# Sixteen-expert transformer kernel: one expert's down product split, a lighter residual, a turned branch, and small moves in order at the start, the merge and the last norm

## The reference, cut to what matters

```
mod = silu(c) @ w_ada + b_ada                     # 9 rows of 1024
h = x + 0.5*gt1 * swiglu(modulate(rms(x), sh1, sc1))          # 1024 -> 2*2816 -> 1024
h = h + gt2 * token_mixing(modulate(rms(h), sh2, sc2))        # pooling + dilated attention
h = h + 0.5*gt3 * swiglu(modulate(rms(h), sh3, sc3))
x = rms(h) * g_final
for l in range(2):
    mix = concat(retention, sliding window, latent attention) @ w_out[l]
    x = layer_norm(ALPHA * x + mix)               # ALPHA = 4 ** 0.25
    # router: best of 4 groups of 4 experts, then its 2 best experts
    y = sum over experts of gate * (silu(x@Wg) * (x@Wu)) @ Wd  # 16 experts, 1024 -> 2*256 -> 1024
    x = layer_norm(ALPHA * x + y)
```

## Time and profile before

| | |
|---|---|
| median of 3 runs | 1162.05 us (1161.95 to 1162.21) |
| the profiled execution, its own time | 1163.61 us |
| its span, first to last record | 1161.8 us |
| granted TensorE clock, mean | 0.985 of full speed |
| instructions | 25234 |
| TensorE busy | 95% of the span |
| VectorE, ScalarE, GpSimd busy | 76%, 54%, 8% |
| moved by DMA | 271.95 MB, mean 234 GB/s |

### The profile page before, as it was taken

How to read it: one execution, slowest core, us unless ns; L and a number is a source line. 1 busy time by engine, 2 the same in 40 slices (tenths; PEclk the granted TensorE clock), 3 DMA queues, 4 the chain that set the end, 5 groups by cost and what they waited for, 6 DMA issues and landing times.

```text
span 1161.8 us, 25234 instructions
## 1 busy us (share of the span) xinstructions
PE 1106.2 (95%) x10870; PEld 850.9 (73%) x10870; DVE 879.8 (76%) x1109; ACT 629.2 (54%) x782; POOL 90.2 (8%) x104
## 2 busy tenths in 40 slices
PE   4899999999999899999999999999999999999995
PEld 4777776698787487777688785887759777588772
DVE  4799799789775775556667857999956775799994
ACT  1554344453465554344466446777746644677762
POOL 1115511071000100000000000000000000000000
PEclk9799999899999999999999999999999999999997
DMA  9999799466544577665464225599985333479970
GB/s 341 371 369 374 245 351 357 145 223 201 187 167 161 171 251 267 217 217 154 141 199 148 75 72 222 206 383 407 381 264 168 112 109 99 194 279 387 399 317 36
DMA packets 134430, 271.95 MB, mean 234 GB/s; under 512 B 9396, under 2 KB 98072, under 8 KB 126008
## 3 DMA queue, kind: packets, MB, share of 16 engines
q1 hardware_dynamic: 123960, 231.79, 56.4%
q0 software_dynamic: 7904, 29.25, 7.1%
q10 hardware_dynamic: 2464, 9.44, 2.1%
HBM read 269.41 MB, written 1.05 MB: 233 GB/s over the span
## 4 chain that ended last, share of the span: by engine, by line
PE 72%; DVE 14%; ACT 7%; DMA 4%; issue 3%; ACTq 0%; SPq 0%; DVEq 0%
PE ps L750 57%; DVE wlo L470 7%; ACT whi L445 2%; DMA area<-in_w_ada_dram 2%; PE ps L1642 2%; DMA raw<-in_w_in_dram 1%; PE ps L888 1%; PE ps L1238 1%; PE ps L1268 1%; PE ps L906 1%; PE ps L1278 1%; DVE x L2262 1%; PE ps L1522 1%; PE ps L1075 1%; PE ps L1267 1%
## 5 line engine op out<-in xcount | busy, mean ns | idle before, releaser
L470 DVE SCALAR_TENSOR_TENSOR wlo<-raw,whi 128x2048 f16<-128x2048 f32 (+4 forms) x212 | 466.1, 2231 | 49.2 <-ACT whi L445 48.4
L445 ACT ACTIVATE whi<-raw 128x2048 f16<-128x2048 f32 (+4 forms) x212 | 384.6, 1848 | 26.2 <-DMA raw<-in_w_ffn_in_dram 10.2
L750 PE MATMUL ps<-uhi,whi 128*128 128x256 f16 (+2 forms) x1328 | 330.8, 261 | 0.9 <-DVE ulo L2317 0.4
L750 PE MATMUL ps<-ulo,whi 128*128 128x256 f16 (+2 forms) x1328 | 330.6, 261 | 0.0
L750 PE MATMUL ps<-uhi,wlo 128*128 128x256 f16 (+2 forms) x1328 | 330.5, 261 | 0.0
L750 PE MATMUL ps<-whi,hreg 128*128 128x512 f16 (+1 forms) x656 | 204.8, 381 | 0.2 <-DVE area L2897 0.2
L750 PE MATMUL ps<-area,whi 128*128 128x96 f16 (+2 forms) x2168 | 154.9, 210 | 3.2 <-ACT area L2157 3.2
L750 PEld LDWEIGHTS ps<-area,whi 128*128 128x128 f16 (+2 forms) x2168 | 145.4, 99 | 15.4 <-issue 9.0
L750 PE MATMUL ps<-area,wlo 128*128 128x96 f16 (+2 forms) x1084 | 149.4, 210 | 0.0
L750 PEld LDWEIGHTS ps<-uhi,whi 128*128 128x128 f16 (+1 forms) x1328 | 130.8, 98 | 23.4 <-issue 9.0
L750 PEld LDWEIGHTS ps<-ulo,whi 128*128 128x128 f16 (+1 forms) x1328 | 130.6, 98 | 15.4 <-issue 1.7
(11 more groups left out here) (361 smaller groups left out, 1428.0 us busy)
## 6 DMA issues: line engine op xcount, KB each, us to landing
raw<-in_exp_w_gate_up_dram SPq DMA_DIRECT2D x64, 1024.0 KB, 7.6
raw<-in_w_ffn_in_dram SPq DMA_DIRECT2D x44, 1024.0 KB, 7.3
raw<-in_w_in_dram SPq DMA_DIRECT2D x34, 1024.0 KB, 7.1
area<-in_w_ada_dram POOLq DMA_DIRECT2D x48, 512.0 KB, 7.3
raw<-in_w_ffn_out_dram SPq DMA_DIRECT2D x22, 1024.0 KB, 8.0
raw<-in_exp_w_down_dram SPq DMA_DIRECT2D x22, 1024.0 KB, 7.8
raw<-in_w_out_dram SPq DMA_DIRECT2D x12, 1024.0 KB, 5.5
x<-in_exp_w_down_dram SPq DMA_DIRECT2D x6, 1024.0 KB, 5.5
```

Of the source, the lines that this page charges most:

```text
L445: act.activation(whi[:, u.slot, 0:n], raw[:, u.slot, 0:n], ACT.Copy, scale=SW)\
L470: dve.scalar_tensor_tensor(out=wlo[:, u.slot, 0:n], in0=raw[:, u.slot, 0:n], scalar=SW, in1=whi[:, u.slot, 0:n], op0=ALU.mult, op1=ALU.sub ...
L750: last = pe.matmul(o, st, mv, start=start and i == 0, stop=stop and i == 2, skip_group_check=True)
```

## The change

- **A, expert 14.** WHOLE loses expert 14: its down weights come as one more 1 MB unit of the ring in each layer, with a hi and a lo part and float16 matmuls. Expert 15 gets place 3 in WHOLE.
- **B, residual.** The factor is S/SX, which one float16 number holds exactly; ALPHA is divided out of what is added to it, and of the epsilon. Sixteen matmuls per tile instead of 24.
- **C, start.** The three broadcasts go to the pool queue behind its wait for ada_pe >= 2. SP waits for the second block's third piece in the order of loading (`ada_in[1][1]`) before the first two weight units. On PE `ada_direct(1)` comes before `transposes(0)`.
- **D, merge.** The lo part of mixing unit 26 (`unit1(23)`) comes after j = 1 of the merge on DVE, and not before j = 0; the hi part of unit 27 (`unit1(24)`) after j = 1 on ACT, and not after j = 3. Five filler matmuls stand before the second `token_transposes`.
- **E, router.** Twenty filler matmuls become 6; 4 more stand after the first gather. ACT gathers after one hi part instead of four; DVE gathers before `gates()`. PE's branch is turned: `sparse()` is the If body, `dense()` the Else body. The 8 fillers behind the branch become 9 at the end of `sparse()`.
- **F, last norm.** The last layer makes no xn: DVE takes (x - mean) * lng on four halves of 512 columns straight from PSUM, then reciprocal, times it plus lnb per half. The output is stored in four halves.

```diff
-WHOLE = (3, 7, 11, 14, 15)
+WHOLE = (3, 7, 11, 15)
...
-    small[:, C_EPSLN + 1] = LN_EPS * S * S
+    small[:, C_EPSLN + 1] = LN_EPS * S * S / (ALPHA * ALPHA)
...
-            sp.dma_start(posi, a["positions"][0].partition_broadcast(P)).then_inc(rows_in, 16)
-            sp.dma_start(sinks[:, :], a["swa_sinks_2"].rearrange("l h -> (l h)").partition_broadcast(P)).then_inc(rows_in, 16)
-
-            sp.dma_start(rbias[:, :], a["router_bias_2"].partition_broadcast(P)).then_inc(rows_in, 16)
-
             def phase(ph):
+                if ph is ffn1:
+                    sp.wait_ge(ada_in[1][1], 16)
...
             for t in range(TT):
-                sp.wait_ge(x_new, 12 + t + 1)
-                sp.dma_start(out[0, t * P:(t + 1) * P, :], x[:, t, :]).then_inc(out_done, 16)
-            sp.wait_ge(out_done, 32)
+                for hf in range(2):
+                    c = slice(hf * HALF, (hf + 1) * HALF)
+                    sp.wait_ge(x_new, 12 + 2 * t + hf + 1)
+                    sp.dma_start(out[0, t * P:(t + 1) * P, c], x[:, t, c]).then_inc(out_done, 16)
+            sp.wait_ge(out_done, 64)
...
             pool.wait_ge(ada_pe, 2)
+            pool.dma_start(posi, a["positions"][0].partition_broadcast(P)).then_inc(rows_in, 16)
+            pool.dma_start(sinks[:, :], a["swa_sinks_2"].rearrange("l h -> (l h)").partition_broadcast(P)).then_inc(rows_in, 16)
+            pool.dma_start(rbias[:, :], a["router_bias_2"].partition_broadcast(P)).then_inc(rows_in, 16)
...
                                 pe.wait_ge(mod_cols, 4)
+                                if q == 1:
+                                    stay_warm(5, 7)
                                 token_transposes(q, 1)
...
-                    for i, (st, mv) in enumerate(((uhi, res_hi), (ulo, res_hi), (uhi, res_lo))):
-                        pe.matmul(o, st[:, k, xs], mv, start=k % 4 == 0 and i == 0, stop=False, skip_group_check=True)
+                    for i, st in enumerate((uhi, ulo)):
+                        pe.matmul(o, st[:, k, xs], res_one, start=k % 4 == 0 and i == 0, stop=False, skip_group_check=True)
...
-            pe.wait_ge(diag_made, 3)
+            ada_direct(1)
+            pe.wait_ge(diag_made, 2)
             transposes(0)
-            ada_direct(1)
...
-                stay_warm(20, 0)
+                stay_warm(6, 0)
...
                     first_gather()
+                    stay_warm(4, 7)
...
                     scatter(3)
+                    if l < LAYERS - 1:
+                        stay_warm(9, 7)
...
-                with pe.If(count > SLOTS):
+                with pe.If(count < SLOTS + 1):
+                    sparse()
+                with pe.Else():
                     dense()
-                with pe.Else():
-                    sparse()
                 if l < LAYERS - 1:
-                    stay_warm(8, 7)
                     token_transposes(2 * l + 4, 0)
                     stay_warm(9, 7)
...
                                ACT.Copy).then_inc(m_hi, 1)
+                if j == 1:
+                    unit1(24)
             act.activation(flag[:, 6:7], zero8[:, 0:1], ACT.Sqrt)
-            for i in range(24, N_MIX):
+            for i in range(25, N_MIX):
                 unit1(i)
...
-                act.activation(mixhi[:, 2 + p, :], ps[:, 6, 0:T], ACT.Copy, scale=SX).then_inc(yo_hi, 1)
+                act.activation(mixhi[:, 2 + p, :], ps[:, 6, 0:T], ACT.Copy, scale=SX / ALPHA).then_inc(yo_hi, 1)
...
-                emit(4)
+                emit(1)
                 gather(0)
+                emit(3)
...
                 for t in range(TT):
                     token_std(2 * l + 1, t)
-                    token_norm(2 * l + 1, t)
+                    if l < LAYERS - 1:
+                        token_norm(2 * l + 1, t)
...
-            unit = np.float32(ALPHA * S / SX)
-            hi = np.float16(unit)
-            for i, value in enumerate((1.0, float(hi), float(np.float16(unit - np.float32(hi))))):
+            for i, value in enumerate((1.0, S / SX)):
                 dve.tensor_scalar(diag[:, i, :], ident, value, None, ALU.mult).then_inc(diag_made, 1)
...
             mix_out_lo(3)
-            unit1(23)
             for j in range(4):
...
                                   mhi[:, 2 * j:2 * j + 2, :], ALU.subtract).then_inc(m_lo, 1)
+                if j == 1:
+                    unit1(23)
...
+                gather(0)
                 gates()
-                gather(0)
                 emit(1)
...
             for t in range(TT):
-                dve.wait_ge(xn_made, 14 + t + 1)
-                dve.wait_ge(xa_made, 12 + t + 1)
-                link(dve.tensor_tensor(x[:, t, :], xn[:, t, :], lng, ALU.mult))
-                dve.tensor_tensor(x[:, t, :], x[:, t, :], lnb, ALU.add).then_inc(x_new, 1)
+                dve.wait_ge(var_made, 2 * (2 * LAYERS - 1) + t + 1)
+                for hf, c in enumerate(halves):
+                    ins = dve.scalar_tensor_tensor(out=x[:, t, c], in0=ps[:, 2 * t + hf, :], scalar=stat[:, 8 + 4 * t:9 + 4 * t],
+                                                   in1=lng[:, c], op0=ALU.subtract, op1=ALU.mult)
+                link(ins)
+            for t in range(TT):
+                dve.wait_ge(rms_made, 2 * (2 * LAYERS + 3) + t + 1)
+                link(dve.reciprocal(stat[:, 4 + t:5 + t], stat[:, 2 + t:3 + t]))
+                for c in halves:
+                    dve.scalar_tensor_tensor(out=x[:, t, c], in0=x[:, t, c], scalar=stat[:, 4 + t:5 + t], in1=lnb[:, c],
+                                             op0=ALU.mult, op1=ALU.add).then_inc(x_new, 1)
```

24 lines of the change are left out of this document (14 added, 10 removed).

## The result

The changed kernel took **1148.89 us** (median of 4 runs, 1148.26 to 1150.29) beside 1162.0 us for the kernel before (median of 4, 1156.76 to 1162.21). Over the runs of both the ratio is 0.990, 95% interval 0.987 to 0.9929. Six later runs of the changed kernel gave 1147.11 us and 0.9869 (0.985 to 0.9888). So by these ratios the change is worth 12 to 15 us, where 19.1 were forecast: right in sign, too high in size. The predicted range of 1136 to 1150 us is 0.978 to 0.9896 of the time before: the first ratio lies just outside it, the later one inside, and the interval of the first takes in both sides.

The account below looks back on a forecast made before the run. PE, busy 95% of the span, was taken to bound the kernel, with DMA full and DVE 90% busy in the experts. Terms summed to -19.1 us off 1162.05, giving 1143.0 us; range 1136 to 1150.

Parts of the forecast that it names:

- C, start: At the kernel's start: columns for the first product near 37.4 us against 39.62, -2.3 us; bounds -3.6 and +1.4.
- Rival 3: Start does not gain: modulation's second block no faster alone, unit 0 late; +1.4 for -2.3, 1146.7 us; chance 0.12.
- D, merge and clock: Lo parts after the merge end near 390.6, -1.9 us; fillers keep the clock for transposes before FFN2, -1.5 us.
- B, residual: Eight fewer matmuls per tile, -0.45 us each tile: -1.8 in the mixers, -0.9 in each expert stage.
- E, router: At the router: branch costs 0.1 to 0.2 us, first gather from 726.3, -3.5 us per layer; bounds 0 and -3.7.
- The cover in the experts: In the expert stages: DVE's lead of 3.9 us is gone, new waits +0.5 us per layer; bounds 0 and +3.5.
- Rival 1: Experts bound by DVE or DMA: another 1.5 us per layer comes back, 1146.0 us; chance 0.15.
- The jump: End of layer 0's sparse body: jump over the dense body delays the next transposes, +1.1 us; bounds 0 and +3.3.
- A and F: Expert 14's split product -0.85 us per layer, layer 0's wait -0.7; last norm -2.0, last store -0.5.
- Rival 5: Slower: fewer router fillers let the clock fall to 1.2 GHz through the experts; about 1239 us; chance 0.03.

Follow-up runs that it names:

- b1: The kernel before with part C alone: 1161.84 us beside 1162.64, ratio 0.9994 (0.9977 to 1.0011).
- b2: The kernel before with the branch turned alone, its 20 fillers and 8 behind the branch kept: 1169.31 us, ratio 1.0059.
- c3: The changed kernel without the five fillers ahead of the transposes before FFN2: 1147.45 us.
- c2: The changed kernel with the lo part of expert 1's down weights cut to 128 of 2048 columns in both layers: 1143.04 us, ratio 0.9838.
- a1: The changed kernel run again, unaltered: 1146.75 us, ratio 0.9876.
- c1: The changed kernel with DVE's halves product before the sums in FFN1's tenth chunk and expert 1's down weights kept float32: 1143.19 us, ratio 0.9838.
- b3: The changed kernel with DVE's halves product before the sums in FFN1's tenth chunk and three group outputs before the next lo part: 1145.91 us.
- a4: The changed kernel with TensorE's untaken dense body cut to one matmul: 1144.64 us beside 1146.75.
- d2: The kernel of c1 in five rounds beside the changed kernel: 1141.96 us beside 1147.11, ratio 0.9825.

## Why the prediction was wrong, step by step

The sum was 19.1 us and the two spans differ by 13.4. In this pair of traces the missing 5.7 are 2.3 at the start, 2.3 in layer 0's experts, 2.1 in layer 1 and 0.75 at the jump, less 1.8 that the merge, the router and expert 14 gave beyond their terms. Two terms failed: the start's -2.3, taken as kept to the end, and the experts' cover, +0.5. The 0.2% that the text gave a measurement were too few as well: the first interval reaches 0.3% to each side.

- **C, start** (-2.3, got 0 in this pair, a little over 1 us in the mean of the traces; b1: 0.9994). The step that failed is the cover, not the arithmetic of the transfers. The fold starts at 32.99 where 32.7 were worked out. That the first product is 4.35 us earlier, and not 2.3, has two other reasons: the fold takes 2.26 us at clock 1.00 where it took 3.57 at 0.50, and the lo part does not hold the columns, since unit 0 is there at 30.84 and not at 33.2. (PE's transposes were not done before the fold, as the text has it: they run from 29.54 to 33.19, and the fold follows them.) But the text followed PE alone from there: it never asked whether DVE, 76% busy over the span, had the gain too. DVE lost 2.75 of its 4.36 us between 42 and 58 us, waiting for hi parts whose weights had not come (DMA share 1.06), and was 1.68 us earlier at the tenth chunk, with 2.9 us of modulation sums ahead of what ACT and PE wait for. Rival 3's outcome (no gain of the start) came true, by another cause than its own.
- **D, merge and clock** (-3.4, got -4.14). Right: the lo parts end at 390.0 (forecast 390.6), the first transposes are 2.5 us sooner, the second take 1.09 us. The clock's 1.5 us hold for this pair of traces; without the fillers the clock falls in three of four traces (the kernel before, b2 and c3, but not b1), so part of this hit is luck of the pair.
- **B, residual.** 16 matmuls in 0.89 us, as forecast.
- **E, router** (-3.5, got -4.33 in layer 0). The branch is 0.08 us where 0.1 to 0.2 was expected, and ACT's earlier gather saved a further 0.9 us behind it, which the text had counted as nothing. b2 shows how much of this hangs on the parts beside the branch.
- **The cover in the experts** (+0.5 per layer, got a wait of 2.56 us at expert 5 in each, and a stretch of low clock behind it in one): the term that was most wrong. The lead was read right (3.9 us against 4.4 gained), but the new wait was taken as the difference of the two at one lo part. DVE was gapless from the gather to expert 5, and the first group's output stands behind a 2.3 us lo part there. Rival 1, at 0.15, named DVE's pace or DMA, with 1.5 us per layer more; c2 shows that it is DVE and not DMA.
- **The jump** (+1.1, got +1.85). Mechanism right, size low: 4.94 us where the price of the old branch, 3.58, was taken. It starts 0.98 us before the scatter's end (0.4 was taken), and varies from 3.5 to 5.9 us; from the last scatter to the transposes the eleven traces need 0.4 to 2.8 us more than the kernel before, 1.7 in the mean.
- **A and F** as forecast: -1.82 for -1.55 in layer 0, -0.84 for -0.85 in layer 1, -2.5 for -2.5 at the end. In F the four SBUF halves took 0.71 us each and not 0.62; -2.0 had been taken for a sum that gave 2.3, and hit.

In layer 1 the wait at expert 5 is followed by 3.4 us at half clock in this trace (windows from 1057.90: 0.51) and in layer 0 not; a1 has it the other way round. Such stretches are placed differently in each trace; that they are what spreads the runs is likely, not shown. Rival 5's mechanism (idle, then a low clock through the experts) did not come: no low stretch in an expert stage was longer than about 3.4 us.

## What to carry to other kernels

When a change gives TensorE a few microseconds, follow the engines beside it to the next place where TensorE waits for one of them: up to there the gain that survives is the smaller of the two shifts (1.68 and not 3.87 us at 196.69), not TensorE's. Ask also what sets the other engine's shift; here it was first weights still on their way, then a transfer that a third engine issued late. A 2 us part taken off that engine ahead of the wait (c1, at 0.85 us of TensorE's own time) brought 2.4 us in the median, a neater order of what is left (b3) nothing. And a branch should fall through where TensorE is waited for, with work already queued where the far jump stands.

## What had not been expected of the hardware

- The same idle does not always bring the low clock. After 3.10 us of idle at 194 us the clock was 0.50 in a1; after 2.92 us at the same place it was 1.00 in a4, which had no low stretch ahead of the last norm. Of the nine traces with this wait (2.34 to 3.65 us) seven had the low clock behind it. Windows, first a1, then a4:

```profile
197.30:200.60 3.30, 3.30 (x17) 2.34 (x16) 3.12 (x5) 3.30 (x4) 1.08 (x2) 0.50 1.07 377
```

```profile
197.30:200.60 3.30, 3.30 (x31) 2.96 (x32) 3.12 (x5) 3.30 (x4) 1.03 (x2) 1.00 1.06 372
```

What decides it is open.
- A jump to a near target takes 0.17 us and one over the dense body 3.5 to 5.9 us, and the time of the far one differs from execution to execution (layer 0: 3.54 us in c3, 4.94 in the first trace, 5.86 in d2; layer 1: 3.29 to 3.87 us). In the first trace the DMA share is 0.60 while layer 0's jump runs and 0.02 in layer 1's (3.29 us). Whether the transfers lengthen it was not tried.
